# Storing a mixture-of-experts unit's results with one transfer into four column blocks

## The reference

```python
for e in range(N_EXPERTS):                 # 16 experts, D_EXPERT = 512
    he = jax.nn.silu(h @ w_gate[e]) * (h @ w_up[e])
    y = y + combine[..., e:e + 1] * (he @ w_down[e])
```

## Time and profile before

| | before |
|---|---|
| median of three runs | 878.61 us |
| profiled execution, its own time | 880.11 us |
| its span, first to last instruction | 878.2 us |
| PE busy / DVE busy / ACT busy | 750.6 / 413.0 / 153.3 us |
| mean of all DMA | 346 GB/s |
| expert stages (first to last unit) | about 320 to 565 us and 630 to 866 us |

### The profile page before, as it was taken

One profiled execution on the slowest core, in us unless ns is written; L12 is line 12 of the kernel. 1 busy time (PEld: TensorE's weight loads), 2 busy tenths in 40 slices (PEclk: granted clock), 3 DMA queues, 4 the chain that ended last, 5 costly groups with the idle time before them and its releaser, 6 DMA issues.

```text
span 878.2 us, 19193 instructions
## 1 busy us (share of the span) xinstructions
PE 750.6 (85%) x7530; PEld 432.8 (49%) x7531; DVE 413.0 (47%) x1079; ACT 153.3 (17%) x334; POOL 32.7 (4%) x58
## 2 busy tenths in 40 slices
PE   8999999997988999985649985799999679696674
PEld 4544647453654455643325653374566445373342
DVE  3268899988897662221011341533622213122335
ACT  4121100224773030000000010230300100000001
POOL 0200000011000000000000001000000000000000
PEclk9999999998998999989788998899999879898988
DMA  9998997899503689999999899997789999999961
GB/s 337 359 386 300 376 348 265 321 386 384 203 1 109 262 320 421 374 366 416 422 421 421 349 422 417 396 411 307 303 344 421 417 418 422 421 422 421 419 275 50
DMA packets 81779, 303.77 MB, mean 346 GB/s; under 512 B 9072, under 2 KB 16288, under 8 KB 57072
## 3 DMA queue, kind: packets, MB, share of 16 engines
q1 hardware_dynamic: 67456, 282.49, 81.0%
q0 software_dynamic: 3552, 12.59, 3.7%
q10 hardware_dynamic: 10704, 7.75, 2.8%
HBM read 291.39 MB, written 14.68 MB: 349 GB/s over the span
## 4 chain that ended last, share of the span: by engine, by line
PE 49%; DMA 21%; DVE 18%; SPq 5%; issue 5%; ACT 2%; ACTq 0%; DVEq 0%; POOL 0%
DMA raw<-in_w_up 17%; PE bank L1924 17%; PE bank L1938 7%; DVE bias L934 5%; PE bank L1905 4%; PE bank L1846 3%; PE bank L1719 3%; SPq L485 3%; PE bank L1729 3%; PE bank L2132 3%; DMA ring<-in_w_in 3%; DVE arena L934 1%; DVE small L1114 1%; SPq L466 1%; PE bank L2100 1%
## 5 line engine op out<-in xcount | busy, mean ns | idle before, releaser
L1924 PE MATMUL bank<-raw,arena 128*32 128x256 f32 x3392 | 224.8, 418 | 75.1 <-DMA raw<-in_w_up 44.7
L1924 PEld LDWEIGHTS bank<-raw,arena 128*32 128x32 f32 x3392 | 128.1, 119 | 165.4 <-issue 117.9
L1437 DVE TENSOR_TENSOR arena<-arena,bank 128x128 f32<-128x128 f32 x53 | 15.2, 287 | 279.6 <-ACT arena L832 279.6
L1938 PE MATMUL bank<-raw,arena 128*32 128x256 f32 x1696 | 107.5, 390 | 12.6 <-issue 12.6
L1938 PEld LDWEIGHTS bank<-raw,arena 128*32 128x32 f32 x1696 | 62.3, 112 | 48.1 <-issue 20.1
L832 ACT ACTIVATE arena<-bank 128x128 f32<-128x128 f32 x53 | 14.7, 277 | 352.7 <-PE bank L1924 352.6
L1729 PE MATMUL bank<-ring,arena 128*128 128x512 f32 x160 | 69.7, 594 | 0.0
L1905 PE MATMUL bank<-arena 128*32 128x256 f32 x912 | 60.8, 380 | 7.5 <-DVE arena L1404 7.5
L934 DVE SCALAR_TENSOR_TENSOR bias<-ring,small,bias 128x512 f32<-128x512 f32 x77 | 57.9, 752 | 2.7
L1729 PEld LDWEIGHTS bank<-ring,arena 128*128 128x128 f32 x160 | 30.1, 190 | 37.2 <-issue 36.4
L934 DVE SCALAR_TENSOR_TENSOR arena<-ring,small,arena 128x512 f32<-128x512 f32 x63 | 47.4, 752 | 2.2
(11 more groups left out here) (268 smaller groups left out, 808.6 us busy)
## 6 DMA issues: line engine op xcount, KB each, us to landing
raw<-in_w_gate SPq DMA_DIRECT2D x64, 1024.0 KB, 20.9
raw<-in_w_up SPq DMA_DIRECT2D x64, 1024.0 KB, 22.3
raw<-in_w_down SPq DMA_DIRECT2D x64, 1024.0 KB, 22.8
ring<-in_ada_w SPq DMA_DIRECT2D x24, 2048.0 KB, 14.8
ring<-in_w_in SPq DMA_DIRECT2D x7, 2048.0 KB, 13.9
unit_results<-arena ACTq DMA_DIRECT2D x220, 32.0 KB, 5.8
ring<-in_w_out SPq DMA_DIRECT2D x2, 2048.0 KB, 23.3
ring<-in_w_fnet SPq DMA_DIRECT2D x2, 2048.0 KB, 18.3
```

The costliest lines, as they stand in the source:

```text
L1924: ins = mm(ps[4][j * S:(j + 1) * S, 0:2 * FW].rearrange("p (m n) -> p m n", m=2), xT[:, k, :], w[:, k % 4, :, j * FW:(j + 1) * FW], start= ...
L1938: ins = mm(ps[5][j * S:(j + 1) * S, 0:XW], hT_e[:, k, :], w[:, k % 2, j * XW:(j + 1) * XW], start=(k == 0), stop=(k == KF - 1))
```

## The change

One transfer takes the place of the four that `store_y` issued. The source is all 128 partitions of a place. The destination is the same 32 rows of the table, walked as column block, row, column: 4 x 32 x 256. The semaphore counts are divided by JN = 4 accordingly.

```diff
@@ fetch_results
-                pool.wait_ge(L[l]["y_stored0"], (NE // 2) * 16 * JN)
-                pool.wait_ge(L[l]["y_stored1"], (NE // 2) * 16 * JN)
+                pool.wait_ge(L[l]["y_stored0"], (NE // 2) * 16)
+                pool.wait_ge(L[l]["y_stored1"], (NE // 2) * 16)
@@ store_y
                     act.wait_ge(E["y_ready"], n + 1)
-                    for j in range(JN):
-                        act.dma_start(yg[bass.ds(at, S), j * XW:(j + 1) * XW], ys[j * S:(j + 1) * S, place, :]
-                                      ).then_inc(E[f"y_stored{place}"], 16)
+                    act.dma_start(yg[bass.ds(at, S), :].rearrange("s (j x) -> j s x", j=JN), ys[:, place, :]
+                                  ).then_inc(E[f"y_stored{place}"], 16)
@@ end of the stored experts, ScalarE
-                act.wait_ge(E["y_stored2"], act.snap(odd, min_val=1, max_val=MAX_UNITS) * (16 * JN))
-                act.wait_ge(E["y_stored3"], act.snap(even, min_val=1, max_val=MAX_UNITS) * (16 * JN))
+                act.wait_ge(E["y_stored2"], act.snap(odd, min_val=1, max_val=MAX_UNITS) * 16)
+                act.wait_ge(E["y_stored3"], act.snap(even, min_val=1, max_val=MAX_UNITS) * 16)
@@ result, VectorE
-                    dve.wait_ge(E[f"y_stored{place}"], stores * (16 * JN))
+                    dve.wait_ge(E[f"y_stored{place}"], stores * 16)
@@ before the late experts, VectorE
-                        dve.wait_ge(E["y_stored1"], (NE // 2) * 16 * JN)
+                        dve.wait_ge(E["y_stored1"], (NE // 2) * 16)
```

## The result

The changed kernel takes 954.54 us (median; 953.42 to 956.47) beside 880.34 us for the kernel before (875.47 to 882.79): 1.0854 times as long, interval 1.0809 to 1.0898. The profiled execution has a span of 954.6 us where the one before had 878.2, 76.4 us more. Split at the layers: up to layer 0's first SiLU +2.7 us, from there to layer 1's first SiLU +44.3 (352.5 against 308.2), from there to the end +29.3 (271.8 against 242.5). Lines of the changed kernel are one lower: L818 is the store, L831 SiLU, L1431 `result`, L1436 the product, L1425 `turn_h`, L1923 and L1937 the unit's matmuls.

A forecast was written before the change was run, and what follows sets the result against it. The weight stream was taken to bound both expert stages, except in runs of units bound by TensorE. Issues -2.4, overload +45.5, longer landing +8 and late fetch +7 gave +58 on 878.6: 937 us, range 890 to 960.

The forecast's parts named there:

- B: Long runs of units: stores on four engines land later, so `result` waits for places; +8 us, a quarter of 32.
- C: Layer ends: the last store lands later and delays the fetch; +5 us in layer 0, +2 in layer 1, +7 in all.
- A: Weight stream: each of 49 stored units costs the four loaded engines 1.12 us more; +45.5 us (36 to 55).
- the issues: ScalarE issues one store DMA per unit in place of four; a quarter of 3.2 us on the chain remains, -2.4 us.
- The cut over four engines: `store_y`: the destination's outer 4 lets only four engines carry 32 KB each, where 16 carried 8 KB; 7404 ACT packets.
- Rival 1: `store_y`: the transfer still spreads over 16 engines, so only issuing gains 2.4 us; 876 us, chance 0.12.
- the credit of 9.4: Taken off the overload's cost where DMA engines stood idle: 4.5, 2.7 and 2.2 us.
- Rival 2: Store transfers use four engines, but the limit is shared, so a unit costs 0.37 us more; 892 us, chance 0.06.
- Rival 3: Waiting for places becomes the bound: 21 further units take 10 us, not 6.04, +84 us; about 1000 us, chance 0.05.
- the six weight stretches: Chain pieces of 18.05 to 31.83 us that are only a weight transfer on its way; forecast to grow.
- GB/s falls to 380, share below 0.95: Sign of being right: in stretches full before, the rate falls from 420 to about 380 GB/s, mean share below 0.95.
- The clock: TensorE's granted clock, 0.87 to 0.90 in full stretches, falls further with more idle time, costing nothing while weights are last.

The follow-up runs named there:

- added transfers: Kernel before plus 26 unawaited 128 KB transfers on SP's queue: cut over four engines 905.01 us (1.0266), over 16 engines 890.05 us (1.0109).

## Why the prediction was right in direction, and what it missed

937 us was forecast, 954.5 measured: slower by 74 us against 58. It lies within the stated 890 to 960 us, and some of that is luck, since two errors point opposite ways. The waits for stores, B and C, were put at 15 us and are 32 to 38; the rest, A and the issues, was put at 43 and is 36 to 42.

- **The cut over four engines**: shown, by 7404 packets, by the steps of the semaphores, and by the version over 16 engines that has no slowdown. Rival 1 is out.
- **Issues, -2.4 us**: L0 of the version over 16 engines is 2.4 us shorter. Agrees, but it is one profile of each.
- **A, +45.5 us (36 to 55)**: its size holds or is somewhat high. With the waits short or gone, the differences of 36.1 and 41.8 us hold A with a little of C, less the issues; that A is as large beside 8 KB packets is not shown by them. The added transfers give 0.58 us each for the extra, so 28 us for 49. Between 28 and 42 us; which, these runs don't settle. The pace of the four late increments in the changed kernel itself, 16.1 us an expert with one store against 15.2, gives 0.9 us a store where A has 1.12: 44 us for 49, 35 with the credit of 9.4 (an estimate from these rows). The limit belongs to the engine and the stream waits for it, as the step said: twelve engines run 14.9 us an expert and the four do not. Rival 2 (0.37 us a unit, 18 us less credit) is not excluded by the added transfers, but by the other figures.
- **B, +8 us (0 to 32): the step that failed, by its size.** "I take a quarter" was the mistake, and the bound was one too. 74.2 less the 36.1 or 41.8 leaves 32 to 38 us for the waits for stores, against 8 for B and the 7 of C. Its mechanism was the right one: 33 packets taking turns, 14 us for an isolated store (14.3 to 14.8 measured), 10 us for each one queued, `turn_h` and `down` behind `result`. Three things were left out of the count. First, the three preset stores, which stand ahead of the first group's: 30 us of queue, and a stretch of 36.62 us on the chain (though only 6.6 us went when they were taken away, since the next waits grew). Second, the first two places of an expert and the end of the stage wait too: 19.30 and 20.11 us at 549 and 569 us, one store after the other. Third, the argument that "while TensorE waits the loaded engines work off what A has already charged" took waiting as nearly free. The traces show otherwise: while TensorE stands, the slots fill up, and then the queue is idle at a share of 0.19.
- **C, +7 us (+5 in layer 0)**: from layer 0's last SiLU to layer 1's first it is 81.4 us before and 92.8 after, +11.4. With 4 KB weight packets it is 81.6 before and 82.0 after. The fetch was late because the last two stores were queued one behind the other, so most of the 6 us more are B again. Its place was right: POOL's fetch, then `add_fetched` (L1551), idle 7.4 us for it.
- **Rival 3, about 1000 us, 0.05**: its time was not reached, but its mechanism is on the chain for 23% of the span, and the six weight stretches shrank to two, where the forecast had them grow. Beside "stores are quick once the weight queue is dry" (true: 3.3 to 3.8 us for the stores issued from 379 to 391 us) stands that the wait comes while the weight queue is still full. It deserved more chance, at a time between.
- **The check "GB/s falls to 380, share below 0.95"**: wrong from 400 to 500 us (421 GB/s, 1.01), nearly met in layer 1 (391 GB/s, 0.96 from 697 to 895 us, against 419 and 1.02 in the earlier trace rows; the 369 of 650 to 848 us takes in 33 us before the layer's first unit). A weight transfer is issued up to 12 transfers ahead (landing 29 us after issue, one every 2.5 us), so twelve engines run on with later transfers, by up to 11.3 us in layer 0, and the mean hides that each transfer ends late.
- **The clock** fell as forecast: 0.83 from 400 to 500 us, where the earlier trace rows has 0.87 from 380 to 500, and 0.899 in place of 0.938 over the span. TensorE is busy for 759.8 us in place of 750.6; whether any of this reached the end is not shown.

The two terms differ in what would mend them: B goes with fewer packets per engine or smaller weight packets, A only with an even cut. A version faster than both kernels was not run. The one over 16 engines writes rows in another order, and a fetch of these would need four gathers for each of today's; that was not tried, and its whole-time ratio below 1 has two units fewer in it.

## What to carry to other kernels

Before one DMA takes the place of several, count the outermost dimension on both sides, DRAM too: the common cut decides how many engines carry it, and 4 in place of 16 cost 8.5% here, though the bytes and their runs were the same and the instructions fewer. Beside a stream of large packets a small transfer lands after (its packets on one engine) x (the time of one packet of the stream), with 4 to 5 us on top in these runs; compare that with the time until its buffer is wanted, and with everything queued ahead of it, the first stores included. Where such a landing exceeds the producer's period, don't take a fraction of the wait: walk through the queue store by store.

## What the runs showed of the hardware

- A DMA cut over four engines posts the other twelve increments 1.0 to 1.5 us after issue, long before its data land (14.3 us and more beside the weights).
- Turn by turn, whatever the size of the small packets: 33 packets of 1 KB over four engines land in 14.3 to 14.8 us, 33 of 256 bytes over 16 engines in 13.4 to 15.3 us, though the engine moves a quarter of the bytes for them.
- The weight stream in pieces of 4 KB costs the kernel before 1.8%, in pieces of 2 KB 3.6%; the rate from 470 to 500 us is 411 GB/s with 4 KB where the full stretches with 8 KB had 419 to 420.
- The mean share of DMA engines and the GB/s can both read "full" (1.01, 421 GB/s) while four engines are up to 11.3 us behind the other twelve. A transfer's own increments show it: 12 early, 4 late.
